# A decoder block with product-key experts: the gates are scattered into cleared memory by adding indirect transfers instead of being built from one-hot products

## The chip, the cores and the metric

The kernel runs on one core of a Trainium2 chip. A core has five engines with a queue of instructions each: TensorE (PE, with its weight loads PEld), VectorE (DVE), ScalarE (ACT), GpSimd (POOL) and SyncE (SP, which here only issues DMA transfers), and 16 DMA engines that all of them share. Engines wait for each other by semaphores. The metric is the device time of one execution in microseconds, and less is better. All arithmetic is float32; where TensorE is used, a float32 value is split in a high part that the fast matmul format holds and a low part that is the rest, and a product is made of three matmuls (high by high, high by low, low by high).

## The reference

One decoder layer for 512 tokens of width 1024: a mixer (attention and a short convolution), a PEER expert layer, a gate with embeddings, and a final norm. The change lies in the expert layer:

```python
q = jnp.einsum('bsd,dhe->bshe', h, w_q)                       # 8 heads
s1, s2 = q[..., :128] @ k1, q[..., 128:] @ k2                 # 128 keys a side
v1, i1 = lax.top_k(s1, 16); v2, i2 = lax.top_k(s2, 16)
top_s, top_j = lax.top_k(all 16 x 16 sums of v1 and v2, 16)
ids = i1 * 128 + i2 at top_j                                  # of 16384 experts
gates = softmax(top_s)                                        # 8 x 16 a token
act = gelu(h . u[ids]);  out = sum(gates * act * v[ids])
```

A token so picks 8 x 16 = 128 experts. An expert may be picked by two heads of one token, and then its gates add up; within one head the 16 picks are different.

## The kernel before

The tokens are four tiles of 128. For tiles 1 to 3 (384 tokens, `DENSE`) the experts are computed densely: stage U computes h . u for all 16384 experts and 512 tokens, in 128 units of 128 experts; stage V multiplies gelu of the scores by a dense matrix of gates, zero where nothing was picked, and by v, in 128 steps. Tile 0 takes another way: POOL gathers its 128 picked scores a token from memory (`pick`, line 519) and the 128 picked rows of v (`fetch_row`, line 526), and DVE adds the rows, weighted (line 1416).

A unit of U: SP loads its weights into `raw` (4 buffers, 512 KB a load), ACT writes the high part `wh` (line 846), POOL the low part `wl` (line 491; in stage V every third by DVE, line 1405, as `low_by_dve` says), both with 8 slots, so eight units ahead of PE. PE then issues 24 matmuls (line 744), ACT copies the sums out (line 1019) and issues their store to `score_dram`. SP loads `raw` of unit n only when the low part of unit n-4 is written, and PE waits for a unit's low part before its first matmul (`wait_low`).

Beside the first 32 units (`ROUTE_U`) DVE does the routing, one tile after the other (`TILE_ORDER` is 1, 2, 3, 0): the top 16 of the pair sums, the key numbers `chosen`, the softmax. The gate matrix is made in the next 78 units: `chosen` is transposed on PE (line 754), and for 96 quads of four tokens DVE builds one-hot rows of both key numbers (`one_hots`, lines 1347 to 1352), POOL scales one by the low part of the gate (`low_gates`, line 498), PE multiplies the one-hots (4 small matmuls a quad between those of U, line 769), ACT and DVE add the two halves into `stage` (lines 1043 and 1368), and ACT stores 12 chunks of 2 MB to `gate_dram`. In stage V SP brings the gates back, 16 groups of 8 steps, and the scores in pairs of steps; ACT applies gelu (line 1061), DVE multiplies by the gates (line 1381), splits (line 1389) and adds finished outputs to x (line 1399).

Everything is issued in the order in which the functions of each engine are written; no scheduler moves it. POOL's queue in stage V is one low part in two of three steps, 8/7 picks a step until step 97 and 8/7 row fetches a step until step 113, with 16 picks ahead of all of them as soon as U is done.

## Time and profile before

| | us |
|---|---|
| median of 3 runs (range) | 1936.13 (1933.49 to 1937.78) |
| the profiled execution | 1935.26 |
| its span in the trace | 1933.3 |
| PE busy in the span | 1852.7 (96%) |
| DVE, ACT, POOL busy | 1277.3, 754.3, 1135.8 |
| matmuls of stage U and of its gates on the chain of waits | L744 36%, L769 2% |

Busy time of an engine is the sum of its instructions in the trace; an engine that is not busy waits for a semaphore or for its queue. Spans on POOL are rough. The chain of waits is followed back from the last instruction to what released it. The rows themselves stand in a section of their own below.

### The profile page before, as it was taken

The page shows a single profiled execution, that of the slowest core. Times are in us where ns is not written, and L with a number is a line of the kernel's source. Part 1 is how long each engine was busy: PE and PEld are TensorE (multiplying, and loading weights), DVE is VectorE, ACT ScalarE, POOL GpSimd, SP SyncE. Part 2 cuts the span into 40 slices and gives each one's busy share as a digit, 9 for nine tenths or more (in the row PEclk, how much of TensorE's full clock was granted, in tenths as well). Part 3 has the DMA queues.
Part 4 walks back from the last instruction along what each step waited for, and adds up shares of the span by engine and source line. Part 5 has one row for each costly group of instructions (what it writes and reads, how often), then busy time and mean ns, then how long its engine had stood idle before and what let it go on. Part 6 is the DMA issues. An engine that isn't in the chain of part 4 may idle for free.

```text
span 1933.3 us, 24277 instructions
## 1 busy us (share of the span) xinstructions
PE 1852.7 (96%) x9045; PEld 1611.5 (83%) x9045; DVE 1277.3 (66%) x2244; ACT 754.3 (39%) x1190; POOL 1135.8 (59%) x666
## 2 busy tenths in 40 slices
PE   6999999989999999999999999988899989999987
PEld 5777788878888888888888888888899989989976
DVE  6355422357899778888989860137686867787543
ACT  5433322333232344444444442433343434344331
POOL 6322344433354476766767764478888888886420
PEclk9999999989999999999999999999999999999998
DMA  5211122312244435544454546649999999999501
GB/s 195 79 66 66 57 99 95 120 66 88 93 146 149 145 124 211 185 174 174 181 202 174 176 173 240 219 161 317 324 344 335 316 350 331 322 344 374 175 33 44
DMA packets 186484, 360.89 MB, mean 187 GB/s; under 512 B 16384, under 2 KB 122880, under 8 KB 184704
## 3 DMA queue, kind: packets, MB, share of 16 engines
q1 hardware_dynamic: 142304, 231.76, 35.8%
q0 software_dynamic: 22528, 67.19, 9.4%
q10 hardware_dynamic: 21536, 60.40, 8.4%
q8 instruction: 72, 1.18, 0.3%
q14 instruction: 44, 0.36, 0.1%
HBM read 298.44 MB, written 60.82 MB: 186 GB/s over the span
## 4 chain that ended last, share of the span: by engine, by line
PE 74%; POOL 17%; issue 3%; DMA 3%; DVE 2%; ACT 1%; ACTq 0%; SPq 0%; DVEq 0%
PE bank L744 36%; PE bank L552 11%; PE bank L554 10%; PE bank L553 10%; POOL wl L491 7%; POOL picked L519 6%; PE bank L769 2%; DMA raw<-stream 2%; POOL rows_ex L526 2%; POOL gout L526 1%; POOL rows_h L526 1%; PE bank L648 1%; PE bank L668 1%; PE bank L722 1%; PE bank L638 0%
## 5 line engine op out<-in xcount | busy, mean ns | idle before, releaser
L491 POOL TENSOR_TENSOR wl<-raw,wh 128x1024 fp32r<-128x1024 f32 x298 | 737.9, 2478 | 670.8 <-ACT wh L846 669.6
L846 ACT ACTIVATE wh<-raw 128x1024 fp32r<-128x1024 f32 x338 | 356.6, 1056 | 324.4 <-PE bank L554 269.1
L552 PE MATMUL bank<-hh,wh 128*128 128x512 f32 (+1 forms) x1056 | 394.5, 374 | 26.4 <-DVE x L1399 17.5
L744 PE MATMUL bank<-hh,wh 128*128 128x512 f32 x1024 | 400.5, 391 | 0.8 <-ACT scores L1001 0.8
L744 PE MATMUL bank<-hh,wl 128*128 128x512 f32 x1024 | 401.0, 392 | 0.0
L744 PE MATMUL bank<-hl,wh 128*128 128x512 f32 x1024 | 399.7, 390 | 0.0
L554 PE MATMUL bank<-hh,wl 128*128 128x512 f32 (+1 forms) x1056 | 387.7, 367 | 0.0
L553 PE MATMUL bank<-hl,wh 128*128 128x512 f32 (+1 forms) x1056 | 387.4, 367 | 0.0
L552 PEld LDWEIGHTS bank<-hh,wh 128*128 128x128 f32 x1056 | 201.3, 191 | 56.0 <-DVE x L1399 19.4
L744 PEld LDWEIGHTS bank<-hh,wl 128*128 128x128 f32 x1024 | 192.2, 188 | 37.7
L744 PEld LDWEIGHTS bank<-hl,wh 128*128 128x128 f32 x1024 | 192.4, 188 | 36.9
L744 PEld LDWEIGHTS bank<-hh,wh 128*128 128x128 f32 x1024 | 192.9, 188 | 34.4 <-ACT scores L1001 1.0
L554 PEld LDWEIGHTS bank<-hh,wl 128*128 128x128 f32 x1056 | 201.1, 190 | 22.8
L553 PEld LDWEIGHTS bank<-hl,wh 128*128 128x128 f32 x1056 | 201.3, 191 | 20.2
L552 PE MATMUL bank<-act_h,wh 128*128 128x384 f32 x512 | 177.2, 346 | 20.0 <-DVE x L1399 19.0
L1043 ACT ACTIVATE stage<-bank 128x256 f32<-128x256 f32 x192 | 108.5, 675 | 224.3 <-PE bank L769 224.3
L553 PE MATMUL bank<-act_l,wh 128*128 128x384 f32 x512 | 175.9, 343 | 0.0
L554 PE MATMUL bank<-act_h,wl 128*128 128x384 f32 x512 | 175.7, 343 | 0.0
L1019 ACT ACTIVATE gout<-bank 128x512 f32<-128x512 f32 x128 | 78.9, 617 | 216.9 <-PE bank L744 216.9
L1347 DVE TENSOR_TENSOR hot<-iota_nk,i1T 128x512 fp32r<-128x512 f32 x96 | 114.1, 1189 | 74.5 <-PE bank L769 74.4
L519 POOL DMA_INDIRECT picked<-score_dram,score_at x128 | 138.5, 1082 | 30.8 <-issue 28.5
L1405 DVE TENSOR_TENSOR wl<-raw,wh 128x1024 fp32r<-128x1024 f32 x40 | 78.1, 1953 | 102.6 <-ACT wh L846 102.6
(211 smaller groups left out, 2569.7 us busy)
## 6 DMA issues: line engine op xcount, KB each, us to landing
raw<-stream SPq DMA_DIRECT2D x338, 512.0 KB, 3.7
score_dram<-gout ACTq DMA_DIRECT2D x128, 256.0 KB, 2.5
gate_dram<-stage ACTq DMA_DIRECT2D x12, 2048.0 KB, 7.5
gate<-gate_dram SPq DMA_DIRECT2D x16, 1536.0 KB, 12.7
score_in<-score_dram SPq DMA_DIRECT2D x64, 384.0 KB, 10.5
x<-xT SPq DMA_DIRECT2D x4, 512.0 KB, 5.6
picked<-score_dram,score_at POOLq DMA_INDIRECT x128, 6.1
outT<-outb SPq DMA_DIRECT2D x8, 256.0 KB, 2.1
```

The source lines that it names most:

```text
L491: nc.gpsimd.tensor_tensor(wl[:, n % SL, :], raw[:, n % RAW, :], wh[:, n % SL, :].bitcast(F32), ALU.subtract).then_inc(lo_done, 1)
L519: nc.gpsimd.indirect_dma_start(picked[:, k:k + 1], None, score_list, bass.IndirectOffsetOnAxis(ap=score_at[:, k:k + 1], axis=0)).then_inc( ...
L526: nc.gpsimd.indirect_dma_start(vrow[k % ROWS], None, row_list, bass.IndirectOffsetOnAxis(ap=row_at[:, k:k + 1], axis=0)).then_inc(rows_in[ ...
L552: nc.tensor.matmul(out, ah, bh, start=start, stop=False)
L553: nc.tensor.matmul(out, ah, bl, start=False, stop=False)
L554: return nc.tensor.matmul(out, al, bh, start=False, stop=stop)
L744: last = nc.tensor.matmul(psum[u % 2][:], w(weights, U_DENSE + u, c), tokens[c][:, :], start=c == 0 and which == 0, stop=c == DC - 1 and w ...
L846: nc.scalar.activation(wh[:, n % SL, :], raw[:, n % RAW, :], ACT.Copy).then_inc(hi_done, 1)
L1019: nc.scalar.activation(gout[:, u % 4, :], psum[u % 2][:], ACT.Copy).then_inc(early_done, 1)
L1043: out = nc.scalar.activation(stage[:, chunk % 2, :, at:at + 2].rearrange("p a t -> p t a"), parts[:, :, 0, :], ACT.Copy)
L1347: nc.vector.tensor_tensor(equal, keys_q, i1T[:, at].unsqueeze(2).to_broadcast([P, QUAD, NK]), ALU.is_equal).then_inc(equal_ready, 1)
L1405: nc.vector.tensor_tensor(wl[:, n % SL, :], raw[:, n % RAW, :], wh[:, n % SL, :].bitcast(F32), ALU.subtract).then_inc(low_own, 1)
```

## The change

The gates no longer go through PE. SP clears a new array in memory, `gates` (128 x 128 x 384 floats, 25 MB), by 48 transfers of 512 KB from a tile of zeros that POOL sets; three of them stand ahead of each of the 16 loads `raw` of units U_DENSE-2 to U_DENSE+13. DVE turns the picks of a dense tile into addresses (`gate_at`) and keeps the gates (`gate_val`). POOL then issues 384 indirect transfers (3 tiles x 8 heads x 16 picks): each writes 128 single floats, one a token, and adds them to what is there. The order is `HEAD_ORDER`; before the first transfer of a head POOL waits until all transfers of the head before it, so far as issued, have landed (a semaphore for each head), since two heads may add to one element. Two transfers follow each low part of U from unit 11 to unit 31, and the other 342 stand at five a unit from unit 32. In that stretch, 72 units (`SCATTER_FREE`), the low parts of U are DVE's, by `low_by_dve`; POOL takes them up again with the low part of unit 112.

Removed are the transposes, the one-hots, the small matmuls and the copies to `stage`. In stage V gates and scores come in pairs of steps into four buffers each (the gates of a pair lie in one piece of 3 KB a partition, those of a group before lay in twelve of 1 KB), a step earlier than the scores before; the rows of tile 0 have 8 buffers for 6 and are added 5 steps after their fetch for 4.

```diff
@@ -57,18 +57,16 @@
 EARLY = GROUPS - 1
 HB = 4
 DENSE = T - P
-GATE_BUFS = 2
 SC = 2
-SCORE_BUFS = 3
+PAIR_BUFS = 4
 ROUTE_U = 32
-TAIL_U = 18
 GELU_BANKS = 3
 OUT_BANKS = 3
 TILE_ORDER = (1, 2, 3, 0)
 BATCH = 16
 BATCHES = HK // BATCH
...
+ZERO = 1024
+ZEROS = NK * DENSE // ZERO
+DENSE_TILES = TILE_ORDER[:-1]
+HEAD_ORDER = [(0, 0), (0, 1)]
+for _h in range(PH):
+    HEAD_ORDER += [(1, _h), (2, _h)] + ([(0, _h + 2)] if _h + 2 < PH else [])
+SCATTER_U = 11
+SCATTER_FREE = 72
+def heads_before(i, h):
+    return sum(head == h for _, head in HEAD_ORDER[:i])
+def scatters_at(u):
+    def begun(u):
+        slow = 2 * max(0, min(u, ROUTE_U) - SCATTER_U)
+        return min(len(HEAD_ORDER) * TOPK, slow + 5 * max(0, u - ROUTE_U))
+    return range(begun(u), begun(u + 1))
...
-    return U_V0 + SL <= n < U_PLE and n % 3 == 0
+    return (U_DENSE + ROUTE_U + SL <= n < U_DENSE + ROUTE_U + SCATTER_FREE + SL
+            or U_V0 + SL <= n < U_PLE and n % 3 == 0)
...
+        gates = nc.dram_tensor("gates", (P, NK, DENSE), F32, kind="Internal").ap()
...
+            def load_pair(h):
+                if h >= PAIR_BUFS:
+                    sp.wait_ge(w_done, SC * (h - PAIR_BUFS + 1))
+                elif h == 0:
+                    for head in range(PH):
+                        sp.wait_ge(scattered[head], 16 * TOPK * (TT - 1))
                 for b in range(SC * h, SC * (h + 1)):
                     sp.wait_ge(score_kept[b % 4], 16 * (b // 4 + 1))
-                sp.dma_start(score_in[:, h % SCORE_BUFS],
-                             score_dram[SC * h:SC * (h + 1), :, P:].rearrange("a b t -> b a t")).then_inc(score_back[h % SCORE_BUFS], 16)
+                sp.dma_start(score_in[:, h % PAIR_BUFS],
+                             score_dram[SC * h:SC * (h + 1), :, P:].rearrange("a b t -> b a t")).then_inc(score_back[h % PAIR_BUFS], 16)
+                sp.dma_start(gate[:, h % PAIR_BUFS], gates[:, SC * h:SC * (h + 1), :]).then_inc(gate_in[h % PAIR_BUFS], 16)
...
+            def clear_gates(i):
+                if i == 0:
+                    sp.wait_ge(zero_set, 1)
+                sp.dma_start(gates_flat[:, ZERO * i:ZERO * (i + 1)], zeros[:]).then_inc(zero_out, 16)
             for n in range(N_UNITS):
                 m = n - U_V0
-                if m in (-3, 2):
-                    load_gates((m + 3) // 5)
-                if 8 < m < NK and m % GB == GB - 4 and m // GB + 1 < GROUPS:
-                    load_gates(m // GB + 1)
-                if -2 <= m < NK - 2 and m % SC == 0:
-                    load_scores((m + 2) // SC)
+                for i in range(ZEROS):
+                    if U_DENSE - 2 + i // 3 == n:
+                        clear_gates(i)
+                if -3 <= m < NK - 3 and m % SC == 1:
+                    load_pair((m + 3) // SC)
...
-            def low_gates(q):
...
-            for n in range(U_DENSE + ROUTE_U + SL):
-                if n == U_DENSE + ROUTE_U + SL - 2:
-                    for q in range(2):
-                        low_gates(q)
+            gate_list = gates.rearrange("b a t -> (b a t)").unsqueeze(1)
+            def scatter(i):
+                r, h = HEAD_ORDER[i // TOPK]
+                if i % TOPK == 0:
+                    pool.wait_ge(gate_ready, r + 1)
+                    if i == 0:
+                        pool.wait_ge(zero_out, 16 * ZEROS)
+                    if h >= 1:
+                        pool.wait_ge(scattered[h - 1], 16 * TOPK * heads_before(i // TOPK, h - 1))
+                k = TOPK * h + i % TOPK
+                nc.gpsimd.indirect_dma_start(gate_list, bass.IndirectOffsetOnAxis(ap=gate_at[:, r, k:k + 1], axis=0),
+                                             gate_val[:, r, k:k + 1], None, compute_op=ALU.add).then_inc(scattered[h], 16)
+            for n in range(U_PQ + SL):
                 low(n)
-            for q in range(QUADS):
-                if q + 2 < QUADS:
-                    low_gates(q + 2)
-                for u in units_ended(q):
-                    low(U_DENSE + u + SL)
-            for n in range(U_DENSE + NK - TAIL_U + SL, U_V0 + SL):
+            pool.wait_ge(unit_used, U_PQ)
+            nc.gpsimd.memset(zeros[:], 0.0).then_inc(zero_set, 1)
+            for n in range(U_PQ + SL, U_DENSE + SL):
                 low(n)
+            for u in range(NK):
+                low(U_DENSE + u + SL)
+                for i in scatters_at(u):
+                    scatter(i)
...
-            def chosen_transposed(r):
...
             pe.wait_ge(sc_out, N_PQ)
-            for u in range(ROUTE_U):
-                for r in range(TT - 1):
-                    if CHOSEN_AT[r] == u:
-                        chosen_transposed(r)
+            for u in range(NK):
...
-            def token_gates(q, k):
...
-            pe.wait_ge(quad_out, QUADS)
...
+                picks = gate_val[:, r, :] if tt in DENSE_TILES else pick_g[:]
+                nc.vector.tensor_tensor(picks.rearrange("p (h k) -> p h k", h=PH), top[:],
                                         gsum[:, 0, :].unsqueeze(2).to_broadcast([P, PH, TOPK]),
                                         ALU.mult).then_inc(chosen_ready, 1)
-            mine = chosen[:, (TT - 1) % 2]
-            dve.wait_ge(chosen_ready, 3 * TT)
-            link(nc.vector.scalar_tensor_tensor(out=picked[:], in0=mine[:, 0, :], scalar=float(NK), in1=mine[:, 1, :],
-                                                op0=ALU.mult, op1=ALU.add))
-            dve.wait_ge(consts2, 6)
+                dve.wait_ge(chosen_ready, 3 * (r + 1))
+                first, second = chosen[:, r % 2, 0, :], chosen[:, r % 2, 1, :]
+                if tt in DENSE_TILES:
+                    link(nc.vector.scalar_tensor_tensor(out=picked[:], in0=second, scalar=float(NK), in1=first,
+                                                        op0=ALU.mult, op1=ALU.add))
+                    at = tt - 1
+                    nc.vector.tensor_scalar(gate_at[:, r, :], picked[:], float(DENSE), token[:, at:at + 1], ALU.mult,
+                                            ALU.add).then_inc(gate_ready, 1)
...
-            def one_hots(q):
...
+            dve.wait_ge(pick_ready, 2)
+            def low(n):
+                dve.wait_ge(hi_done, n + 1)
+                nc.vector.tensor_tensor(wl[:, n % SL, :], raw[:, n % RAW, :], wh[:, n % SL, :].bitcast(F32),
+                                        ALU.subtract).then_inc(low_own, 1)
+            for n in range(U_DENSE, U_V0 + SL):
+                if low_by_dve(n):
+                    low(n)
```

POOL's order around the end of routing, before: a low part of U (`wl<-raw,wh`) and one or two scaled one-hots (`hot<-hot,gT_l`) a unit.

```order
L491 TENSOR_TENSOR wl<-raw,wh 128x1024 [waits hi_done] x110
L498 TENSOR_TENSOR hot<-hot,gT_l 128x4x128 [waits high_ready] x2
L491 TENSOR_TENSOR wl<-raw,wh 128x1024 [waits hi_done] x2
L498 TENSOR_TENSOR hot<-hot,gT_l 128x4x128 [waits high_ready] x2
L491 TENSOR_TENSOR wl<-raw,wh 128x1024 [waits hi_done]
L498 TENSOR_TENSOR hot<-hot,gT_l 128x4x128 [waits high_ready]
```

The same place now, and the end of the scatter (`gates<-gate_val,gate_at` is one transfer of 128 floats; `x15` counts repeats):

```order
L484 TENSOR_TENSOR wl<-raw,wh 128x1024 [waits hi_done]
L499 DMA gates<-gate_val,gate_at 6291456x1 x2
L484 TENSOR_TENSOR wl<-raw,wh 128x1024 [waits hi_done]
L499 DMA gates<-gate_val,gate_at 6291456x1 x8
L499 DMA gates<-gate_val,gate_at 6291456x1 [waits gate_ready]
L499 DMA gates<-gate_val,gate_at 6291456x1 x15
L499 DMA gates<-gate_val,gate_at 6291456x1 [waits scattered1,gate_ready]
L499 DMA gates<-gate_val,gate_at 6291456x1 [waits scattered6,gate_ready]
L499 DMA gates<-gate_val,gate_at 6291456x1 x15
L484 TENSOR_TENSOR wl<-raw,wh 128x1024 [waits hi_done] x24
L518 DMA picked<-score_dram,score_at 128x1 [waits scattered5,scattered6,scattered4,scattered7,scattered3,score_kept0,scattered2,score_kept1,scattered1,score_kept2,scattered0,score_kept3,unit_used,pick_ready]
L518 DMA picked<-score_dram,score_at 128x1 x15
L484 TENSOR_TENSOR wl<-raw,wh 128x1024 [waits hi_done]
```

The one-hots have gone; after the low part of unit 39 there stand 342 transfers with no low part among them, in 16s with a wait at the head of each, then 24 low parts in a row (units 112 to 127 and the first eight of V) and the gathers of stage V as before.

DVE's order behind routing, before: one-hots and the additions to `stage`.

```order
L1340 TENSOR_TENSOR gT_l<-gT,gT_h 128x384 [waits chT_out,pick_ready]
L1347 TENSOR_TENSOR hot<-iota_nk,i1T 128x4x128 [waits dve_own]
L1349 TENSOR_TENSOR hot<-iota_nk,i2T 128x512
L1352 TENSOR_TENSOR hot<-hot,gT_h 128x4x128 [waits equal_ready]
L1347 TENSOR_TENSOR hot<-iota_nk,i1T 128x4x128 [waits quad_done]
L1349 TENSOR_TENSOR hot<-iota_nk,i2T 128x512
L1352 TENSOR_TENSOR hot<-hot,gT_h 128x4x128 [waits equal_ready]
L1368 TENSOR_TENSOR stage<-bank,stage 128x2x128 [waits high_out]
L1368 TENSOR_TENSOR stage<-bank,stage 128x2x128
```

The same place now:

```order
L1276 SCALAR_TENSOR_TENSOR picked<-chosen 128x128 [waits chosen_ready]
L1277 TENSOR_SCALAR row_at<-picked 128x128 [waits dve_own]
L1278 TENSOR_SCALAR score_at<-picked,token 128x128
L1284 TENSOR_TENSOR wl<-raw,wh 128x1024 [waits hi_done,pick_ready]
L1284 TENSOR_TENSOR wl<-raw,wh 128x1024 [waits hi_done] x71
L1300 TENSOR_TENSOR bank<-bank,gate 128x384 [waits gate_in0,gelu_done] x2
L1308 TENSOR_TENSOR act_l<-bank,act_h 128x384 [waits wcopy]
```

DVE goes from routing to 72 low parts of U and from there to stage V; the one-hots and additions have gone.

## Rows read from the trace of the kernel before

**Rows 1.** The page: busy time of the engines, and the chain by line.
```profile
PE 1852.7 (96%) x9045; PEld 1611.5 (83%) x9045; DVE 1277.3 (66%) x2244; ACT 754.3 (39%) x1190; POOL 1135.8 (59%) x666
PE bank L744 36%; PE bank L552 11%; PE bank L554 10%; PE bank L553 10%; POOL wl L491 7%; POOL picked L519 6%; PE bank L769 2%; DMA raw<-stream 2%; POOL rows_ex L526 2%; POOL gout L526 1%; POOL rows_h L526 1%; PE bank L648 1%; PE bank L668 1
```

**Rows 2.** Busy time by stretch (columns as its head line says).
```profile
core 0: us, PE busy (x) PEld busy (x) DVE busy (x) ACT busy (x) POOL busy (x), PEclk, DMA share, GB/s
430.00:525.00 95.00, 94.24 (x472) 79.93 (x471) 75.17 (x486) 29.98 (x44) 35.52 (x15) 1.00 0.26 89
800.00:1000.00 200.00, 200.00 (x951) 167.24 (x951) 174.12 (x203) 92.91 (x147) 141.05 (x74) 1.00 0.51 183
1160.00:1259.00 99.00, 99.00 (x437) 81.67 (x435) 9.02 (x18) 35.34 (x53) 43.08 (x18) 1.00 0.66 225
1375.00:1392.00 17.00, 12.60 (x64) 12.60 (x65) 12.97 (x19) 5.76 (x10) 14.47 (x12) 0.90 0.93 309
1400.00:1500.00 100.00, 95.57 (x541) 94.93 (x540) 75.91 (x102) 42.73 (x71) 86.40 (x66) 0.98 0.99 338
```

**Rows 3.** The chain in order of time around stage U: start us, us, what.
```profile
510.13 49.24 PE bank L744 x216
559.69 32.68 PE bank L744 x144
...
1259.02 0.73 issue
1259.75 0.41 PE bank L552
```

**Rows 4.** Timeline of POOL: start us, us, engine line op, [idle before <-releaser].
```profile
561.02 2.40 POOL L491 TENSOR_TENSOR wl<-raw,wh 128x1024 fp32r<-128x1024 f32 x1 [2.99 <-ACT wh L846]
...
1268.77 0.94 POOL L519 DMA_INDIRECT picked<-score_dram,score_at  x1 [0.30 <-issue]
```

**Rows 5.** L519 and L526, POOL's gathers: durations (min/median/max ns) and L519's landings.
```profile
L519 POOL DMA_INDIRECT picked<-score_dram,score_at x128: 940/958/1774, 1264.8 to 1729.7; - x128
DMA to landing us min/median/max: 2.4/6.1/8.6
...
L526 POOL DMA_INDIRECT gout<-stream,row_at x44: 933/940/1496, 1294.5 to 1791.0; - x44
```

**Rows 6.** Timeline of POOL and DVE in stage V.
```profile
1273.76 0.94 POOL L519 DMA_INDIRECT picked<-score_dram,score_at  x1 [0.30 <-issue]
1273.84 1.23 DVE L1405 TENSOR_TENSOR wl<-raw,wh 128x1024 fp32r<-128x1024 f32 x1 [3.31 <-ACT wh L846]
...
1296.29 3.93 DVE L1405 TENSOR_TENSOR wl<-raw,wh 128x1024 fp32r<-128x1024 f32 x1 [3.01 <-ACT wh L846]
1299.29 1.77 POOL L519 DMA_INDIRECT picked<-score_dram,score_at  x1 [0.16 <-issue]
```

**Rows 7.** Timeline of DVE: end of routing.
```profile
653.29 0.22 DVE L1337 COPY pick_g<-chosen 128x128 f32<-128x128 f32 x1
```

**Rows 8.** Timeline of PE behind a wait in stage V.
```profile
1379.40 0.44 PE L552 MATMUL bank<-act_h,wh 128*128 128x384 f32 x1 [4.99 <-DVE x L1399]
1380.28 0.52 PE L552 MATMUL bank<-act_h,wh 128*128 128x384 f32 x1
1383.33 0.33 PE L553 MATMUL bank<-act_l,wh 128*128 128x384 f32 x1
```

**Rows 9.** The page: DMA issues, with median us to landing.
```profile
gate_dram<-stage ACTq DMA_DIRECT2D x12, 2048.0 KB, 7.5
gate<-gate_dram SPq DMA_DIRECT2D x16, 1536.0 KB, 12.7
score_in<-score_dram SPq DMA_DIRECT2D x64, 384.0 KB, 10.5
```

**Rows 10.** Waits from 1300 to 1760 us: total, times, longest.
```profile
ACT bank L1061 <- DMA score_in<-score_dram: 38.2, 10, 8.8
PE bank L552 <- DVE x L1399: 30.7, 14, 5.0
```

More of the change, by code:

```diff
@@ L69 @@
 BATCHES = HK // BATCH
-ROWS = 6
-ROW_LAG = 4
+ROWS = 8
+ROW_LAG = 5
 U_V0 = U_DENSE + NK
@@ L369, in peer_block_kernel @@
         o_ready = sem("o_ready")
-        score_back = [sem(f"score_back{i}") for i in range(SCORE_BUFS)]
-        gate_in = [sem(f"gate_in{i}") for i in range(GATE_BUFS)]
+        score_back = [sem(f"score_back{i}") for i in range(PAIR_BUFS)]
+        gate_in = [sem(f"gate_in{i}") for i in range(PAIR_BUFS)]
         gelu_done = sem("gelu_done")
@@ L527, in fetch_row @@
                                              bass.IndirectOffsetOnAxis(ap=row_at[:, k:k + 1], axis=0)).then_inc(rows_in[k % ROWS], 16)
-            pool.wait_ge(pick_ready, 3)
+            pool.wait_ge(pick_ready, 2)
             pool.wait_ge(unit_used, U_V0)
-            for par in range(2):
-                pool.wait_ge(stage_out[par], 16 * (CHUNKS // 2))
+            for h in range(PH):
+                pool.wait_ge(scattered[h], 16 * TOPK * (TT - 1))
             for i in range(4):
@@ L764, in _ @@
                         score_chunk(u, c, which)
-            def token_gates(q, k):
-                bank = psum[2 + 2 * (q % 3) + k // 2]
-                small = nc.tensor.matmul(bank[:, k % 2 * 2 * NK:(k % 2 + 1) * 2 * NK], hot2[:, q % HOTS, k, :],
-                                         hot1[:, q % HOTS, k].rearrange("p s n -> p (s n)"), start=True, stop=True)
-                if k == QUAD - 1:
-                    small.then_inc(quad_done, 1)
-            pe.wait_ge(chT_out, 4)
-            for q in range(QUADS):
-                if q >= 3:
-                    pe.wait_ge(quad_out, q - 2)
-                pe.wait_ge(hot_ready, q + 1)
-                first, last = quad_chunks(q)
-                for n in range(3 * (last - first)):
-                    score_chunk(*divmod(first + n // 3, DC), n % 3)
-                    if n % 2 == 1 and n < 2 * QUAD:
-                        token_gates(q, n // 2)
-            for u in range(NK - TAIL_U, NK):
-                for c in range(DC):
-                    for which in range(3):
-                        score_chunk(u, c, which)
-            pe.wait_ge(quad_out, QUADS)
             pe.wait_ge(early_done, NK)
@@ L1074, in high_act @@
                 nc.scalar.activation(act_h[g % 2][:, j, :], psum[3 + b % GELU_BANKS][:, 0:DENSE], ACT.Copy).then_inc(wcopy, 1)
-            for u in range(NK - TAIL_U, NK):
+            for u in range(NK):
+                for r in range(TT):
+                    if EXP_AT[r] == u:
+                        act.wait_ge(top_ready, r + 1)
+                        nc.scalar.activation(top[:], top[:], ACT.Exp).then_inc(gexp, 1)
                 scores_out(u)
@@ L1313, in _ @@
                 for side in range(2):
-                    if side == 0 and r >= 2:
-                        dve.wait_ge(chT_ready, 3 * (r - 1))
-                    elif side == 1:
+                    if side == 1:
                         dve.wait_ge(chosen_ready, 3 * r + 1)
@@ L1335, in _ @@
+            link(nc.vector.scalar_tensor_tensor(out=picked[:], in0=first, scalar=float(NK), in1=second, op0=ALU.mult, op1=ALU.add))
             nc.vector.tensor_scalar(row_at[:], picked[:], float(NK * U_V0), None, ALU.add).then_inc(pick_ready, 1)
             nc.vector.tensor_scalar(score_at[:], picked[:], float(T), token[:, 0:1], ALU.mult, ALU.add).then_inc(pick_ready, 1)
-            nc.vector.tensor_copy(pick_g[:], mine[:, 2, :]).then_inc(pick_ready, 1)
-            dve.wait_ge(pick_ready, 3)
@@ L1356, in _ @@
-            for q in range(HOTS):
-                one_hots(q)
-            for q in range(QUADS):
-                chunk, k = divmod(q, GT // QUAD)
-                dve.wait_ge(quad_done, q + 1)
-                if q + HOTS < QUADS:
-                    one_hots(q + HOTS)
-                dve.wait_ge(high_out, q + 1)
-                for half in range(2):
-                    parts = psum[2 + 2 * (q % 3) + half][:].rearrange("p (t s a) -> p t s a", t=2, s=2)
-                    at = QUAD * k + 2 * half
-                    sums = stage[:, chunk % 2, :, at:at + 2].rearrange("p a t -> p t a")
-                    out = nc.vector.tensor_tensor(sums, parts[:, :, 1, :], sums, ALU.add)
-                out.then_inc(quad_out, 1)
+            dve.wait_ge(pick_ready, 2)
```

131 lines of the change are left out of this document (21 added, 110 removed).

## The prediction

> **What bounds the kernel now.** I read the page first. PE is busy 96% of the span, and of the chain of waits L744, the matmuls of U, is 36% and L769, the small gate matmuls between them, 2%; POOL's lines are 17% [rows 1]. Busy time by stretch then says where POOL counts: in stage U (800 to 1000, 1160 to 1259) PE is busy all the time at full clock and POOL 141 of 200 and 43 of 99 us, so U is PE's. In 1400 to 1500, stage V, PE loses 4.4 us, POOL shows 86.4 us in 66 instructions, and the DMA share is 0.99 [rows 2]. Of the 66 about 15 are low parts of 2.40 and 51 indirect DMAs, each with 0.30 us before it that counts as idle [rows 4]; 86.4 + 51 x 0.30 = 101.7, so POOL's queue is full there. V is POOL's and the DMA engines', and with the same picks and rows it stays so.
>
> The chain in order of time dates stage U: it begins at 510.13, a unit takes 32.68 / 6 = 5.447 us (144 matmuls), and the first matmul of V is at 1259.75, behind an end of U at 1259.02 [rows 3].
>
> **The change part by part.** Where S is the start of U, unit k is needed at S + 5.447 k.
>
> *Off PE.* U now takes 1259.02 - 510.13 = 748.9 us; 128 units with nothing between them take 697.2. Small matmuls and transposes so cost 51.7 us, all on the path, and all of it goes: -51.7.
>
> *The scatter, on POOL.* No add of 128 floats is in the trace. The nearest row is the gather of 128 floats (L519): 0.94 us and 0.30 us to the next [rows 4], 1.245 from start to start; the same addresses, the other direction. From below I allow 1.145 (0.84 us busy, what is left of a gather once VectorE lets it go, below). From above the slowest gather is 1.774 us [rows 5], 2.07 with its gap. I take 1.245, the median's row.
>
> *POOL against the low parts of VectorE.* In the stretch where POOL only scatters, VectorE makes a low part of 1.23 us in each unit. A gather that begins while such a one runs is held: VectorE's low part of 1296.29 ends at 1300.22, and the gather begun at 1299.29 takes 1.77 and ends at 1301.06, 0.84 behind it. One that began before it (1273.76) is not held, and neither is VectorE [rows 6]. Let E be the end of a low part. The held transfer ends at E + 0.84, the next three begin at E + 1.14, 2.39 and 3.63, the one after at E + 4.88, while the next low part runs (E + 4.22 to E + 5.447), and is held again. So POOL gets four transfers into a unit, not the five that the list has. That stays four up to a transfer 0.14 us longer.
>
> The Trainium skill (SBUF — State Buffer, two separate sides) has the pair of ports that both engines share as an exclusive lock for a whole instruction, with a VectorE operation of two SBUF inputs counting only against a GpSimd operation that reads SBUF; by that rule a transfer, which reads its addresses there, is held, and the trace agrees (1.77 for 0.94 us).
>
> *When POOL is done.* Unit 31 ends at S + 174.3; POOL's low part starts about 1.7 us behind a unit's end (561.02, against S + 9 units = 559.2) and takes 2.40 [rows 4], two transfers follow: S + 180.9. VectorE's last low part, of unit 111, is begun behind the end of unit 103 and ends at S + 569.4. In between are 71.3 units with four transfers each, 286. The other 56 take 56 x 1.245 = 69.7: S + 639.1. At the end of the list head 7 of a tile stands right behind head 6 of another and waits until that has landed, 6.1 us [rows 5]; elsewhere 16 transfers lie between, 20 us. The low part of unit 112 takes 2.56 with its gap: S + 647.8. PE needs it at S + 610.1. **PE stalls 37.7 us in front of unit 112.** Everything of the low path is queued behind the scatter: SP's loads from raw 116 on, ACT's high parts, and VectorE, which has no low part left. Afterwards a low part (2.56) is shorter than a unit, so it is one stall.
>
> *The clock.* Behind a wait of 4.99 us, at 1379.40, the matmuls of V take 0.52 us and from 1383.3 on 0.33; the clock of that stretch is 0.90 [rows 2, 8], a time at the lower of the two levels (1.2 of 2.4 GHz). Half of 4 us is lost: +2.0. After 38 us it may be up to twice that.
>
> *Hidden.* Routing ends at 653.3 [rows 7] and gains some 0.5 us a tile for the addresses; VectorE's first low part is asked for at S + 33 x 5.447 + 1.7 = 691.6. In units 11 to 31 POOL has 2.56 + 2 x 1.245 = 5.05 us for 5.447, and eight units of lead: 0, and about 3 us if routing holds transfers. The 48 clears are 25 MB, as the 12 stores of 2 MB were. They fall beside 95 us (430 to 525) in which a DMA share of 0.26 moves 89 GB/s [rows 2]: all of it would be 342, so 253 are free, and the clears want 265. The engines are just full; 1.1 MB, some 3 us, is left over, and a raw load behind three clears (4.5 us) has four units of time: 0, at most 5. Gates and scores in stage V: the same bytes in the same share of 0.99, gates in larger pieces. ACT waited 38.2 us for scores of 10.5 us landing behind group loads of 12.7, and PE 30.7 for the additions [rows 9, 10]; smoother loads can give some back, but POOL's full queue stays. I take 0 and allow -20 to +5.
>
> **Sum**, against the profiled 1935.3: -51.7 + 37.7 + 2.0 = -12.0, so 1923.3. The median shown is 0.9 above that execution: **1924 us**.
>
> **Rivals.**
>
> A. *VectorE does not hold the scatter* (the held gather shown had VectorE's low part itself stretched to 3.93 us; one of 1.23 may hold less). Then 342 x 1.245 = 425.8 us end at S + 606.7, and with landing and low part S + 615.4: a stall of 5.3. 1935.3 - 51.7 + 5.3 + 2 = 1891. For it: a low part of VectorE that starts inside a transfer costs nothing [rows 6], and a transfer of 0.94 fills three quarters of the time. Against it: the hold of 1.77 us is the longest duration of L519 and occurs whenever the start falls in.
>
> B. *An adding transfer costs POOL more than a gather*, the rival on the slow side. The issue may be longer, since the destination is read as well as written. The place is the same, the 342 transfers; it decides from +0.14 us each, where the fourth start of a unit falls behind the next low part and the four come apart. At +0.2 (1.445 apart) starts are at E + 1.34, 2.79 and 4.23, the last is held, so three a unit: 214 by S + 569.4, the other 128 take 185: a stall of 154, and 1935.3 - 51.7 + 154 + 2 = 2040. At +0.15 it is some 80 (1966), at +0.5 some 205 (2090). For it: the price of an add is a number that no row shows, and it counts 342 times. Against it: gathers of 4 bytes and of 4 KB a partition take the same 0.94 [rows 5], so the description, not the bytes, is the price, and up to +0.1 it adds only 56 x 0.1 = 5.6.
>
> The Trainium skill (DMA: Bandwidth & Descriptors, Specifications) has writes under 512 B as a read-modify-write in the DMA engine, and an add is one in any case. By this rule the time until a scatter has landed grows, beyond the 6.1 us of the gathers, and C is what it would do here.
>
> C. *Landing is late.* If 16 adds land only 20 us behind their issue, in place of 6.1, each of the waits at a head that follows two groups later still holds, but the first and the last such wait grow, by 24 us together in the end: 1924 + 24 = 1948. The landings of the gathers, 2.4 to 8.6 with DMA engines full, speak against it [rows 5].
>
> D. The change might leave matmuls on PE: it doesn't; nothing stands between units of U any more, so -51.7 is the firm part.
>
> **How the numbers follow.** Chances: the forecast with its stall (transfer from 0.1 shorter to 0.1 longer than a gather) 0.48; A 0.10; B 0.32; C and late raw loads 0.10. The forecast's own range: stall 32.6 to 44, clock 2 to 4, stage V down to -8: 1911 to 1933. A difference under 0.2% (3.9 us) can't be told from none here. The forecast is faster by more but for its upper end, A is faster, B and C slower: faster 0.53, same 0.08, slower 0.39. The range runs from A to the lower half of B, 1888 to 2045, and leaves 0.03 below and 0.16 above.
>
> **What would show it.** Right: no L769; U units 5.45 us apart at clock 1.00; one wait of PE of 33 to 44 us on POOL's low part, in front of unit 112, with a lower clock behind; scatters of 0.94 us, one in four about 1.4; VectorE's low parts 1.23; a second half of stage V as before. Wrong: scatters over 1.1 us (B), five a unit (A), waits at the heads of more than 10 us (C), ACT waiting for raw from 430 to 530, or a stage V shorter by 15 us, which would make the DMA engines and not POOL its bound.

## The result, and the profile after

The changed kernel takes **2147.5 us** (median of 4, 2144.07 to 2148.76) against 1936.35 for the kernel before beside it (1933.49 to 1937.78): a ratio of 1.1085, with a 95% interval of 1.1069 to 1.1100. The forecast was 1924 with a range up to 2045; the time lies outside it and has the other sign. The profiled execution took 2148.8 us, with a span of 2147.0.

The page after, busy time and the chain by line, answers to [rows 1]. The columns are the same.

```profile
PE 1807.5 (84%) x8652; PEld 1565.9 (73%) x8652; DVE 963.2 (45%) x1840; ACT 651.9 (30%) x994; POOL 1442.8 (67%) x883
...
POOL gates L499 29%; PE bank L551 9%; PE bank L553 9%; PE bank L552 9%; POOL wl L484 9%; PE bank L743 7%; POOL picked L518 6%; POOL rows_ex L525 2%; POOL gout L525 1%; POOL rows_h L525 1%; PE bank L647 1%; PE bank L667 1%; DMA raw<-stream 1
```

PE lost 45 us of work, as it was meant to, but it is busy only 84% of the span. The head of the chain is now POOL's scatter, where it was U's matmuls. The view of that line gives its durations (min/median/max ns) and landings; it answers to [rows 5].

```profile
L499 POOL DMA_INDIRECT gates<-gate_val,gate_at x384: 1552/1556/3813, 579.2 to 1363.7; - x192
...
who waited for it (us, times):
  POOL gates L499: 2.1, 1
...
DMA to landing us min/median/max: 2.9/3.0/3.2
```

One transfer holds POOL for 1.556 us; with the 0.30 to the next that is 1.86 from start to start. The landings are short, and the waits of a head for the head before it add up to one of 2.1 us. Busy time by stretch answers to [rows 2].

```profile
core 0: us, PE busy (x) PEld busy (x) DVE busy (x) ACT busy (x) POOL busy (x), PEclk, DMA share, GB/s
430.00:525.00 95.00, 94.24 (x471) 79.87 (x470) 75.16 (x485) 29.89 (x44) 35.92 (x15) 1.00 0.96 331
711.00:1082.00 371.00, 370.13 (x1633) 306.18 (x1632) 85.87 (x70) 106.78 (x139) 312.36 (x194) 1.00 0.67 153
1120.00:1360.00 240.00, 0.00 (x0) 0.00 (x0) 0.00 (x0) 0.00 (x0) 199.02 (x129) 0.50 0.23 0
1600.00:1700.00 100.00, 92.42 (x519) 89.89 (x518) 76.37 (x96) 39.67 (x66) 86.53 (x65) 1.00 0.96 331
```

The first row is the stretch with the clears: the DMA engines are full (0.96) and PE is busy for the same 94.24 us as before. The second is the stretch where VectorE makes the low parts of U; PE loses nothing. In the third every engine but POOL stands for 240 us. The last is stage V: the DMA share is 0.96 and POOL shows 86.53 us, as before (0.99 and 86.40 in 1400 to 1500 [rows 2]). How the standstill begins and ends is in the timelines of four engines: first PE,

```profile
1113.57 0.39 PE L743 MATMUL bank<-hh,wl 128*128 128x512 f32 x1
1372.46 0.80 PE L743 MATMUL bank<-hh,wh 128*128 128x512 f32 x1 [258.50 <-ACT gout L983]
1373.06 0.63 PE L743 MATMUL bank<-hl,wh 128*128 128x512 f32 x1
1373.48 0.63 PE L743 MATMUL bank<-hh,wl 128*128 128x512 f32 x1
...
1377.75 0.61 PE L743 MATMUL bank<-hh,wh 128*128 128x512 f32 x1
1378.18 0.41 PE L743 MATMUL bank<-hl,wh 128*128 128x512 f32 x1
1378.43 0.40 PE L743 MATMUL bank<-hh,wl 128*128 128x512 f32 x1
```

then POOL,

```profile
1363.67 1.55 POOL L499 DMA_INDIRECT gates<-gate_val,gate_at  x1 [0.30 <-issue]
1364.68 9.81 POOL L484 TENSOR_TENSOR wl<-raw,wh 128x1024 fp32r<-128x1024 f32 x4
```

SP's queue,

```profile
1367.62 7.23 SPq L446 DMA_DIRECT2D raw<-stream  x4
```

and ACT.

```profile
1103.12 0.60 ACT L983 ACTIVATE gout<-bank 128x512 f32<-128x512 f32 x1 [3.89 <-PE bank L743]
1370.87 1.06 ACT L810 ACTIVATE wh<-raw 128x1024 fp32r<-128x1024 f32 x1 [267.15 <-DMA raw<-stream]
1371.83 0.58 ACT L983 ACTIVATE gout<-bank 128x512 f32<-128x512 f32 x1
```

Read from the bottom up: ACT copies a unit of scores out at 1103.12 and then stands in its queue at the high part of a later unit, whose raw tile SP may load only when POOL has made the low part of the unit that held the buffer. POOL's low part stands behind the last transfer, begun at 1363.67. When it is done, SP loads (1367.62), ACT makes the high part (1370.87) and only then the copy-out (1371.83) which frees PE's bank. So PE isn't released by the low part but by ACT, some 5 us behind it. It also stopped one unit sooner than its own low part would have made it: a unit may start only when the copy-out of the unit two before it is done, and the copy-out that ACT owed was that of unit 109. After 258 us of nothing PE runs at the lower clock level (0.50, 1.2 GHz) for about 12 matmuls, 0.427 us apart in place of 0.227.

**Where the 213 us come from.** The profiled executions differ by 2148.8 - 1935.3 = 213.5. Matmuls off PE -51.7; the one wait +258.5; the clock behind it 12 x 0.2 = +2.4; stage V, from the end of U to the last picks' transposes 560.2 us before (1259.02 to 1819.17) and 563.4 after (1467.97 to 2031.37), +3.3. The sum is +212.5; the 1.0 us left over is not placed.

### The profile page after: what moved, and what is told of

It reads as the page before. It is cut to its first block, busy times and chain, and to the rows that moved or that the text cites. A ratio compares the mean times of both kernels' runs of the same rounds, so it can differ in the third digit from the quotient of the medians.

```text
span 2147.0 us, 23217 instructions
## 1 busy us (share of the span) xinstructions
PE 1807.5 (84%) x8652; PEld 1565.9 (73%) x8652; DVE 963.2 (45%) x1840; ACT 651.9 (30%) x994; POOL 1442.8 (67%) x883
## 3 DMA queue, kind: packets, MB, share of 16 engines
q0 software_dynamic: 77824, 67.41, 16.1%
## 4 chain that ended last, share of the span: by engine, by line
POOL 48%; PE 38%; issue 10%; DVE 2%; DMA 1%; ACT 1%; SPq 0%; DVEq 0%; POOLq 0%; ACTq 0%
POOL gates L499 29%; PE bank L551 9%; PE bank L553 9%; PE bank L552 9%; POOL wl L484 9%; PE bank L743 7%; POOL picked L518 6%; POOL rows_ex L525 2%; POOL gout L525 1%; POOL rows_h L525 1%; PE bank L647 1%; PE bank L667 1%; DMA raw<-stream 1%; PE bank L721 1%; DVE bank L1329 1%
## 5 line engine op out<-in xcount | busy, mean ns | idle before, releaser
L484 POOL TENSOR_TENSOR wl<-raw,wh 128x1024 fp32r<-128x1024 f32 x226 | 558.7, 2490 | 460.7 <-ACT wh L810 459.4
L499 POOL DMA_INDIRECT gates<-gate_val,gate_at x384 | 621.6, 1619 | 115.9 <-issue 113.7
L1284 DVE TENSOR_TENSOR wl<-raw,wh 128x1024 fp32r<-128x1024 f32 x112 | 178.0, 1590 | 434.5 <-ACT wh L810 396.6
L1300 DVE TENSOR_TENSOR bank<-bank,gate 128x384 f32<-128x384 f32 x128 | 70.9, 554 | 347.1 <-ACT bank L996 347.1
L518 POOL DMA_INDIRECT picked<-score_dram,score_at x128 | 143.9, 1124 | 31.3 <-issue 29.0
```

The lines of the kernel that those rows point to most:

```text
L484: nc.gpsimd.tensor_tensor(wl[:, n % SL, :], raw[:, n % RAW, :], wh[:, n % SL, :].bitcast(F32), ALU.subtract).then_inc(lo_done, 1)
L499: nc.gpsimd.indirect_dma_start(gate_list, bass.IndirectOffsetOnAxis(ap=gate_at[:, r, k:k + 1], axis=0), gate_val[:, r, k:k + 1], None, com ...
L518: nc.gpsimd.indirect_dma_start(picked[:, k:k + 1], None, score_list, bass.IndirectOffsetOnAxis(ap=score_at[:, k:k + 1], axis=0)).then_inc( ...
L1284: nc.vector.tensor_tensor(wl[:, n % SL, :], raw[:, n % RAW, :], wh[:, n % SL, :].bitcast(F32), ALU.subtract).then_inc(low_own, 1)
L1300: nc.vector.tensor_tensor(bank, bank, gate[:, h % PAIR_BUFS, b % SC, :], ALU.mult).then_inc(w_done, 1)
```

## The experiments

**e1_plain: the same transfer without the add.**

```
-                                             gate_val[:, r, k:k + 1], None, compute_op=ALU.add).then_inc(scattered[h], 16)
+                                             gate_val[:, r, k:k + 1], None).then_inc(scattered[h], 16)
```

> The changed kernel with the 384 scatters as plain writes (no add, so where two heads pick one expert the later gate stands alone); clears, order and waits stay. Theory 1, the add itself makes a transfer dear for POOL (1.56 us against 0.94 for a gather): L499 falls to 0.94 us, the 342 transfers end 342 x 0.62 = 212 us sooner, PE's stall of 258 shrinks to some 50, and the time is 1935 to 1945 us. Theory 2, it is the direction (memory is the indexed side that is written): L499 stays at 1.56 and the time at 2147.

Measured: 1936.42 us (8 runs), ratio to before 1.0002 [0.9987, 1.0016]. The view of the line, and PE's one wait in U:

```profile
L499 POOL DMA_INDIRECT gates<-gate_val,gate_at x384: 954/958/3229, 578.5 to 1151.5; - x192
...
DMA to landing us min/median/max: 2.1/2.4/5.1
```

```profile
1159.84 0.79 PE L743 MATMUL bank<-hh,wh 128*128 128x512 f32 x1 [47.77 <-ACT gout L983]
```

The word "add" alone is 0.60 us of POOL's time per transfer, and 211 us of the kernel's. The order, the addresses and the direction are the same, so the rival that writing by index is dear is out. That e1 takes the time of the kernel before is a coincidence: it saves the same 51.7 us on PE and loses 47.77 in the one wait. What the DMA engines have to do changes too. In a stretch of e1 where nothing runs but the scatter (the columns of the other such rows):

```profile
1120.00:1150.00 30.00, 0.00 (x0) 0.00 (x0) 0.00 (x0) 0.00 (x0) 22.97 (x24) 0.50 0.02 0
```

Their share is 0.02 there, against 0.23 in the row 1120 to 1360 of the adding kernel, though the plain ones follow each other faster (24 started in 30 us, against 129 in 240). By the packets of POOL's queue on the pages (77824 with the add, 34816 in e1, 22528 in e3, which has no scatter) each of the 384 adding transfers is 144 packets and a plain one 32. But full DMA engines aren't what holds POOL: an adding transfer is 1.55 to 1.56 us at a share of 0.23 as at 0.67.

With the price of a gather the rest of the forecast's model can be tested too. Timeline of POOL (first fence) and of VectorE (second) in the stretch with VectorE's low parts:

```profile
900.98 0.96 POOL L499 DMA_INDIRECT gates<-gate_val,gate_at  x1 [0.30 <-issue]
902.24 1.34 POOL L499 DMA_INDIRECT gates<-gate_val,gate_at  x1 [0.30 <-issue]
903.89 0.96 POOL L499 DMA_INDIRECT gates<-gate_val,gate_at  x1 [0.30 <-issue]
905.15 0.96 POOL L499 DMA_INDIRECT gates<-gate_val,gate_at  x1 [0.30 <-issue]
906.41 0.96 POOL L499 DMA_INDIRECT gates<-gate_val,gate_at  x1 [0.31 <-issue]
907.67 1.35 POOL L499 DMA_INDIRECT gates<-gate_val,gate_at  x1 [0.30 <-issue]
```

```profile
901.53 1.23 DVE L1284 TENSOR_TENSOR wl<-raw,wh 128x1024 fp32r<-128x1024 f32 x1 [4.21 <-ACT wh L810]
906.97 1.23 DVE L1284 TENSOR_TENSOR wl<-raw,wh 128x1024 fp32r<-128x1024 f32 x1 [4.21 <-ACT wh L810]
```

The low part runs from 901.53 to 902.76. The transfer begun at 902.24, inside it, ends at 903.58, 0.82 behind it; the one begun before it (900.98) is not held. From 902.24 to 907.67 there are four transfers in one unit of 5.43 us, one of them held: the pattern of the forecast, within 0.03 us.

**e2_half_tokens: the add kept, 64 of the 128 tokens in each transfer.**

```
-                nc.gpsimd.indirect_dma_start(gate_list, bass.IndirectOffsetOnAxis(ap=gate_at[:, r, k:k + 1], axis=0),
-                                             gate_val[:, r, k:k + 1], None, compute_op=ALU.add).then_inc(scattered[h], 16)
+                nc.gpsimd.indirect_dma_start(gate_list, bass.IndirectOffsetOnAxis(ap=gate_at[0:64, r, k:k + 1], axis=0),
+                                             gate_val[0:64, r, k:k + 1], None, compute_op=ALU.add).then_inc(scattered[h], 16)
```

> The changed kernel with each adding transfer over 64 tokens in place of 128 (half of the dense tokens get no gate). If POOL pays by the element, L499 falls from 1.56 to about 0.8 to 1.0 us and the time by 342 x 0.6 to 0.75 = 205 to 257 us, to 1890 to 1945. If it pays by the instruction, L499 stays near 1.56 us and the time near 2147.

Measured: 2101.81 us, ratio 1.0861 [1.0832, 1.0891].

```profile
L499 POOL DMA_INDIRECT gates<-gate_val,gate_at x384: 1403/1407/3662, 581.0 to 1317.0; - x192
```

Half the elements take 1.407 us in place of 1.556: near the expectation of a price by the instruction, and outside both of its times. On a straight line through the two, 0.15 us goes with each 64 elements and 1.26 us is there whatever their number. So most of the price is one per instruction, and smaller transfers are no way out; whether larger ones would be was not run.

**e3_no_scatter: no transfers at all.** The 384 transfers and the waits on them are left out; the clears stay, and SP waits for them in front of the first gates.

```
-                for i in scatters_at(u):
-                    scatter(i)
```

> The changed kernel without its 384 scatters (the dense gates stay zero); clears, DVE's low parts and the rings of pairs stay. It prices all the rest of the change. My forecast's firm part, -51.7 us for the small matmuls and transposes and nothing elsewhere: 1936.4 - 51.7 = 1885 us, PE without a wait in U. Rival, the clears or the new order of loads cost too: over 1892. Rival, the smoother loads shorten stage V: under 1878.

Measured: 1885.68 us, ratio 0.9748 [0.9727, 0.9769], 50 us under before, against 51.7 forecast for the matmuls off PE. Two stretches of it, the clears and late U (columns as above):

```profile
430.00:525.00 95.00, 94.24 (x467) 79.75 (x467) 76.41 (x489) 29.50 (x44) 35.72 (x15) 1.00 0.95 335
1000.00:1200.00 200.00, 200.00 (x884) 165.65 (x883) 24.48 (x28) 64.09 (x90) 52.76 (x23) 1.00 0.52 172
```

This is the floor of the change. Clears, VectorE's low parts and the new loads of gates cost nothing that can be told from none; the 262 us from here up to 2147.5 belong to the scatter.

**e4_lows_to_127: VectorE makes the low parts up to the end of U.** The add stays.

```
-SCATTER_FREE = 72
+SCATTER_FREE = 88
```

> The changed kernel with VectorE making the low parts up to unit 127 (88 units for 72), so that POOL owes PE nothing before stage V. If the stall is in front of the first low part that stands behind the scatter in POOL's queue (seen through ScalarE, which waits for raw 116 and so for SP), it now begins where SP's wait for the last scatter, ahead of raw 125, reaches PE, nine units later: the stall shrinks by 9 x 5.45 = 49 us and the time is 2095 to 2105. If something else ended the stall (the clears, a DMA queue), no change: 2147.

Measured: 2102.86 us, ratio 1.0867 [1.0834, 1.0899]. Its view of waits, and the line of its scatter:

```profile
PE bank L743 <- ACT gout L983: 213.2, 2, 212.4
```

```profile
L499 POOL DMA_INDIRECT gates<-gate_val,gate_at x384: 1551/1555/3809, 578.5 to 1362.6; - x192
```

The scatter ends where it did (last start 1362.6 and 1363.7) and the stall is 46 us shorter, because U is held up 48 us later (1162.1 for 1114.0) and let go 2 us later. So the stall is the end of the scatter less the point at which the program first asks for something behind it, here SP for the first gates of stage V.

**e5_plain_lows_127: both edits, plain writes and low parts to unit 127.**

> Plain writes as in e1_plain (sums of gates over heads are left out) and VectorE's low parts up to unit 127 as in e4. If the time is set by the end of the scatter and by where its end is asked for, the two add up: the stall of 47.8 us in e1 loses up to nine units (49 us), less the holds by 16 more low parts (16 x 0.47 = 7.5): 1936 - 48 + 7 = 1895 us, between 1888 and 1900. If something else had been hidden behind the stall (the landing of 48 clears, loads), it stays over 1910.

Measured: 1893.36 us, ratio 0.9780 [0.9765, 0.9794]; PE's longest wait in U is 5.8 us. With a price of 0.96 and the scatter asked for late, nearly all of the 50 us comes in. This kernel leaves out the sum where two heads of a token pick the same expert; the next two put it back.

**e6_summed_plain: the whole computation with plain writes.** VectorE adds to each head's gate those of the lower heads with the same expert, so that the last write to an address holds the sum; heads are written in ascending order. Routing then takes about 37 us more a tile, so the other marks move, and VectorE makes low parts again up to unit 127. SP waits for the scatter in front of the first gates and no longer in front of the first scores (that edit is not shown).

```
+                    for h in range(PH - 1, 0, -1):
+                        n = TOPK * h
+                        own = slice(n, n + TOPK)
+                        pairs = flat[:, 0:TOPK * n].rearrange("p (k j) -> p k j", k=TOPK)
+                        link(nc.vector.tensor_tensor(pairs, picked[:, own].unsqueeze(2).to_broadcast([P, TOPK, n]),
+                                                     picked[:, 0:n].unsqueeze(1).to_broadcast([P, TOPK, n]), ALU.is_equal))
+                        link(nc.vector.tensor_tensor(pairs, pairs, gate_val[:, r, 0:n].unsqueeze(1).to_broadcast([P, TOPK, n]),
+                                                     ALU.mult))
+                        link(nc.vector.tensor_reduce(same[:], pairs, AX.X, ALU.add))
+                        link(nc.vector.tensor_tensor(gate_val[:, r, own], gate_val[:, r, own], same[:], ALU.add))
...
-ROUTE_U = 32
+ROUTE_U = 41
-SCATTER_U = 11
-SCATTER_FREE = 72
+SCATTER_U = 13
+SCATTER_FREE = 79
-EXP_AT = (7, 13, 18, 23)
+EXP_AT = (7, 18, 29, 40)
```

> A version that computes everything: VectorE adds, for each head, the gates of lower heads of the same token that picked the same expert (compare, multiply, reduce over 16 x 16h pairs, seven heads, some 26 us a tile), and the scatter is of plain writes in the order of heads, so the last write holds the sum. VectorE's low parts begin nine units later (unit 49) and go to 127, the exponentials wait later, and SP waits for the last scatter only in front of the first gates, at step 1 of V. POOL's transfers cost 0.96 + 0.30 us at four a unit, and end near unit 121. Theory 1 (only the price of the add was wrong): PE's stall is under 15 us and the time 1888 to 1905 us, below the kernel before by 1.5 to 2.5%. Rival: VectorE's 78 us more of routing come late for the scatters of tiles 2 and 3 and push POOL's end back by 20 us or more: 1915 to 1930.

Measured: 1930.78 us, ratio 0.9968 [0.9956, 0.9981]: faster than before by 0.3%, but near the rival's time (up to 1930), not the expected one. The rival's mechanism is there only in part. POOL hardly waited for the addresses of a late tile (first fence: us, times, longest), but ACT, whose Exp of a tile stands in its queue in front of copy-outs of U, did wait for VectorE's routing (second):

```profile
POOL gates L505 <- DVE gate_at L1291: 2.9, 2, 2.2
```

```profile
753.14 0.31 ACT L1021 ACTIVATE top<-top 128x128 f32<-128x128 f32 x1 [19.62 <-DVE top L1247]
```

PE lost 38.7 us in U in three waits (4.4 at 680, 11.2 at 754, 23.1 at the end). The first two are behind such an Exp. They also hold up POOL's low parts, and the scatter ended at 1212.9, some 42 us behind the unit 121 of the expectation; how much of that is due to these waits is not shown. Timeline of ACT in front of the last one, and of VectorE:

```profile
1186.14 1.05 ACT L816 ACTIVATE wh<-raw 128x1024 fp32r<-128x1024 f32 x1
1218.18 0.49 ACT L1015 ACTIVATE act_h<-bank 128x384 fp32r<-128x384 f32 x1 [30.99 <-DVE bank L1317]
...
1218.98 0.59 ACT L989 ACTIVATE gout<-bank 128x512 f32<-128x512 f32 x1
```

```profile
1217.58 1.03 DVE L1317 TENSOR_TENSOR bank<-bank,gate 128x384 f32<-128x384 f32 x2 [34.57 <-DMA gate<-gates]
```

ACT has the activations of V's first blocks (L1015) in its queue among the last copy-outs of U (L989). They need the first gates, and the gates need the whole scatter. A wait that belongs to V was standing in U.

**e7_gates_asked_later: e6 with three things asked for later.** No operation is added or taken away. The diff is against e6: first ACT's Exp of two tiles, then SP's loads of gates, then ACT's first eight activations of V (step is the unit less 128, GB is 8).

```
-EXP_AT = (7, 18, 29, 40)
+EXP_AT = (7, 18, 31, 44)
...
-                    load_pair((m + 3) // SC)
-                    for h in ((), (), (0, 1, 2))[(m + 3) // SC] if m < 3 else ((m + 3) // SC,):
+                    h = (m + 3) // SC
+                    if h < PAIR_BUFS or m > GB:
+                        load_pair(h)
+                    if m > GB:
+                        load_gates(h)
+                if m == GB:
+                    for h in range((GB + 3) // SC + 1):
+                        if h >= PAIR_BUFS:
+                            load_pair(h)
                         load_gates(h)
...
-                if step >= -GB:
-                    high_act(step + GB)
-                if step >= -GB - 2:
+                if -GB - 2 <= step < -GB:
                     gelu(step + GB + 2)
+            for b in range(GB):
+                high_act(b)
+                gelu(b + 2)
```

> The version of e6_summed_plain (sums over heads on VectorE, plain writes, whole computation) with three orders changed and no operation. ScalarE's Exp of the third and fourth tile stands behind units 31 and 44 of U, not 29 and 40, since PE stood 4.4 and 11.2 us at 680 and 754 behind ScalarE waiting for them. SP waits for the scatter in front of the raw load of unit 8 of V, not of unit 1, and ScalarE's first eight high parts of activations stand behind unit 127 of U, not behind units 120 to 127, so that only the start of V, and not the last units of U, waits for the gates. Theory: the scatter is POOL's and ends at 1213 as in e6, the first gates come at 1217.6, eight pairs of activation and split take about 1.4 us each, and V begins at 1230 instead of 1250: 1930.8 - 20 = 1911, range 1905 to 1918; U shows no stall over 5 us, but V's first matmul waits about 26 us. Rival: the six pairs of gates and scores loaded at once, and the raw loads behind them, hold V in its first units, or the scatter ends later: 1920 to 1931.

Measured: **1899.45 us** (5 runs), ratio 0.9809 [0.9794, 0.9825]: the whole computation, 1.9% faster than before. Scatter, the first matmul of V, and VectorE at that place:

```profile
L512 POOL DMA_INDIRECT gates<-gate_val,gate_at x384: 954/958/3088, 588.9 to 1200.1; - x192
```

```profile
1215.47 0.39 PE L756 MATMUL bank<-hh,wl 128*128 128x512 f32 x1
1219.10 0.66 PE L564 MATMUL bank<-act_h,wh 128*128 128x384 f32 x1 [3.24 <-DVE act_l L1333]
```

```profile
1217.27 1.03 DVE L1325 TENSOR_TENSOR bank<-bank,gate 128x384 f32<-128x384 f32 x2 [47.35 <-DMA gate<-gates]
1218.39 0.56 DVE L1333 TENSOR_TENSOR act_l<-bank,act_h 128x384 fp32r<-128x384 f32 x1
...
1219.33 0.55 DVE L1333 TENSOR_TENSOR act_l<-bank,act_h 128x384 fp32r<-128x384 f32 x1
```

VectorE waits longer for its gates than in e6 (47.35 against 34.57 us), and it costs nothing, since nothing of U stands behind it. V begins at 1219.1 instead of 1250.3. The time is below the expected range of 1905 to 1918. The expectation let V wait for all eight blocks, at 1.4 us each; V starts with the first, and a block takes 0.94. It also had the scatter end where it did in e6, and it ended 12 us sooner (last start 1200.1 for 1211.9): of the two early waits of U one of 3.0 us is left, and POOL's low parts come sooner too. The expected wait of 26 us in front of V was 3.2, and it is no longer the scatter's:

```profile
1211.13 2.17 SPq L424 DMA_DIRECT2D gate<-gates  x4
```

SP's queue comes to the first gates 10 us behind the end of the scatter. PE's waits in U and in front of V are 38.7 + 0.7 us in e6 and 6.4 + 3.2 here, which is 30 of the 31 us: some 12.5 in the two early waits (15.5 to 3.0), which goes with the Exp, and some 17 at the end of U, which goes with the other two edits together. No run has them apart.

## Why the prediction was wrong

**The scatter, on POOL (the step that failed).** The forecast priced the adding transfer by the gather of 128 floats, 1.245 us from start to start, with 2.07 as its upper bound, and took the lower value because the gathers had one price whatever their bytes. The price was 1.86, inside the bounds and towards the wrong end. e1 shows that it is the add: 0.958 us without, 1.556 with it. (A plain write so costs what the gathers' median says, 0.958 and 1.26 with the gap [rows 5]; 1.245 goes with their shortest, 0.94. That slip is small.) The gathers' equal price says nothing of it, since they have no add. That is rival B (given 0.32), in what it says of the price and at its place. B had been worked out only up to +0.5 us, and the range only up to its lower half, though the step's own upper bound was +0.83. The range was too narrow for the bound that it was meant to take in.

**When POOL is done.** The forecast has POOL done with the scatter at S + 645.2 (S + 639.1, and 6.1 for a landing), PE stopping at S + 610.1 and going on at S + 647.8. S, the first matmul of U, is at 507.92 in e1 and, in the changed kernel, at

```profile
508.68 0.50 PE L743 MATMUL bank<-hh,wh 128*128 128x512 f32 x1 [0.76 <-ACT scores L965]
```

e1 tries the formula at the price that it was filled with. POOL was done at 1152.5, S + 644.6. That it fits so well is in part luck: the later phase, the 342 transfers, began 3 us late and the landing cost 1.9 us and not 6.1. PE stopped at S + 604.2, 5.9 sooner than forecast, and went on at S + 651.9, 4.1 later: a stall of 47.8 against 37.7. These 10 us have nothing to do with the price. PE stops behind unit 110, one unit before the one that the forecast named, and starts again 5 us behind the low part, because it hangs on ACT's copy-out behind a high part behind a raw load. The forecast had named ACT's high parts and SP's loads as "queued behind the scatter" and still let PE run as if only its own operand mattered. So at the price that it took it would still have been 12 us too low: e1 took 1936.4, not 1924.

In the changed kernel POOL was done at S + 856.5, 211.3 us behind the forecast, in two parts. First, the later phase began late. The low part behind which the first two transfers stand, the one behind which the last two of this phase stand (20 units on), and the first of the 342:

```profile
575.89 3.15 POOL L484 TENSOR_TENSOR wl<-raw,wh 128x1024 fp32r<-128x1024 f32 x1 [3.04 <-ACT wh L810]
...
708.16 2.98 POOL L484 TENSOR_TENSOR wl<-raw,wh 128x1024 fp32r<-128x1024 f32 x1
...
715.83 1.56 POOL L499 DMA_INDIRECT gates<-gate_val,gate_at  x1 [0.30 <-issue]
```

A low part and two transfers took 6.61 us on average over these 20 units (the two low parts are 132.27 apart), for a unit of 5.447 and a forecast of 5.05. POOL fell behind, and 715.83 is S + 207.2 against S + 180.9: 26 us. Second, the 342 transfers take 636 us at 1.86, with 12 holds of 1 us and one landing of 2.1 beside them: 649 against 464 forecast, 185 more. Their time by line:

```profile
L499 POOL DMA_INDIRECT gates<-gate_val,gate_at x193 | 312.9, 1621 | 58.6 <-issue 58.6
```

```profile
L499 POOL DMA_INDIRECT gates<-gate_val,gate_at x129 | 200.5, 1554 | 41.1 <-issue 39.0 <-DMA gates<-gate_val,gate_at 2.1
```

(Groups by line in 711 to 1082, with VectorE's low parts on, and in 1120 to 1360; count, busy us, mean ns, idle before.) PE stopped 4.8 us sooner than forecast and went on 4.7 us later behind POOL, much as in e1. 211.3 + 4.8 + 4.7 = 220.8, the difference of the stalls (258.5 and 37.7).

**POOL against the low parts of VectorE: right.** e1 shows four transfers a unit, the held one ending 0.82 behind the low part (0.84 forecast). Rival A, without the hold, is refuted. With the longer transfer the hold hardly matters: 2.8 fit into a unit, and 13 of the 193 in 711 to 1082 were held (the first of them still belongs to the earlier phase). The rule on the shared ports (the Trainium skill, SBUF — State Buffer, two separate sides) agrees with e1's 1.34 us for 0.96. Its other half, that a GpSimd operation which starts first holds VectorE up, doesn't show: the low part of 901.53, begun inside the transfer of 900.98, took its 1.23 us.

**Landing (rival C): refuted.** A scatter landed in 3.0 us with the add and 2.4 without; the waits at the heads are 2.1 us in all. The rule that small writes are a read-modify-write in the DMA engine (the Trainium skill, DMA: Bandwidth & Descriptors, Specifications) has no price for POOL. By it the cost would fall behind the issue, and for plain writes of 4 bytes as for adding ones. In these traces the DMA engines do have more work with the add (a share of 0.23 against 0.02), but it costs the kernel nothing that shows: the adding transfer holds the issuing engine 0.60 us longer, and the landing, counted from the issue, is later by the same 0.6.

**Off PE, hidden work, clock.** -51.7: e3 shows it, 50.1 in the medians beside it and no wait of PE over 1 us in U. Clears and loads at no cost: right, in e3 and in the row 430 to 525; that stretch was forecast just full, and its share is 0.96. Stage V within -20 to +5: +3.3. The clock +2.0, up to twice that after a long wait: 2.4 behind 258 us without a matmul, hardly more than the 2.0 read behind 5 us.

## What to carry to other kernels

An operation that no row shows and that counts hundreds of times is the forecast: take its upper bound through the whole sum, the phases before the critical one too, and let the range reach there. Adding on the way to memory has another price than writing (1.556 us against 0.958 of POOL's time); if the sums can be made beforehand, plain writes may win even at 37 us a tile on another engine, as in e7. And what a late producer costs is its end less the first place that asks for it in *any* queue on the path: e4 and e7 gained 45 and 31 us by asking later, with no work removed (in e7 some 12 of them by asking later for the routing, not for the scatter).

## What the runs showed of the hardware

An indirect transfer of 128 floats from POOL took 0.94 to 0.96 us as a gather [rows 5], 0.958 as a plain write and 1.556 as an adding write; the adding one took 1.407 for 64 floats, so on a line through the two most of it is a price per instruction. With nothing else running the adding transfers kept the 16 DMA engines 0.23 busy, the plain ones 0.02; an adding one of 128 floats was 144 packets, one of 64 floats 80, a plain one of 128 floats 32. The 0.30 us to the next was the same for all. An adding transfer begun inside a low part of VectorE took up to 2.60 us in place of 1.56, a plain one up to 1.37 in place of 0.96. Clears of 25 MB and the weight loads beside them ran at 331 GB/s together, with a DMA share of 0.96, and PE was busy for the same 94.24 of 95 us.
